# The gather's token rows kept in column order, with the stationary operand at every eighth column

## The reference, cut to what matters

```python
def grouped_moe(h, router_w, router_bias, w_gate, w_up, w_down):
    xt = h.reshape(B * T, D)                       # 256 tokens x 1024
    aff = jax.nn.sigmoid((xt @ router_w).astype(jnp.float32))
    ...                                            # 2 experts of 16 for each token, and their shares
    hg = jnp.einsum('nd,edf->nef', xt, w_gate)     # 1024 -> 512 for each expert
    hu = jnp.einsum('nd,edf->nef', xt, w_up)
    act = jax.nn.silu(hg) * hu * gates[:, :, None].astype(hg.dtype)
    out = jnp.einsum('nef,efd->nd', act, w_down)   # 512 -> 1024
```

## Time and profile before

| | us |
|---|---|
| median of 3 runs (1164.02 to 1165.67) | 1165.38 |
| the profiled execution, its own time | 1164.87 |
| its span, first to last instruction | 1163.1 |
| PE busy | 1073.0 (92%) |
| PEld busy | 743.2 (64%) |
| DVE busy | 562.8 (48%) |
| ACT busy | 419.8 (36%) |
| POOL busy | 89.3 (8%) |

### The profile page before, as it was taken

One profiled execution on the slowest core, in us unless ns is written; L12 is line 12 of the kernel. 1 busy time (PEld: TensorE's weight loads), 2 busy tenths in 40 slices (PEclk: granted clock), 3 DMA queues, 4 the chain that ended last, 5 costly groups with the idle time before them and its releaser, 6 DMA issues.

```text
span 1163.1 us, 15867 instructions
## 1 busy us (share of the span) xinstructions
PE 1073.0 (92%) x6103; PEld 743.2 (64%) x6103; DVE 562.8 (48%) x1054; ACT 419.8 (36%) x750; POOL 89.3 (8%) x114
## 2 busy tenths in 40 slices
PE   6999998999999999896999999979889699999995
PEld 5899977899999787674444443358767544444332
DVE  5754375766666556756222222274684722222224
ACT  5355435545455345732111111143474321111111
POOL 1200000000000011510000000011151000000000
PEclk9999998999999998997999999989989899999998
DMA  8743353545554442338999999943241889999993
GB/s 297 253 145 109 100 189 110 181 160 201 185 186 170 139 131 107 110 137 347 421 420 420 420 420 418 418 158 119 78 149 70 361 349 421 418 420 420 420 420 132
DMA packets 81684, 294.55 MB, mean 253 GB/s; under 512 B 7253, under 2 KB 40387, under 8 KB 56915
## 3 DMA queue, kind: packets, MB, share of 16 engines
q1 hardware_dynamic: 79456, 289.29, 64.6%
q10 hardware_dynamic: 1394, 2.18, 0.5%
q0 software_dynamic: 768, 2.19, 0.5%
HBM read 292.59 MB, written 1.05 MB: 252 GB/s over the span
## 4 chain that ended last, share of the span: by engine, by line
PE 78%; DVE 9%; DMA 5%; ACT 5%; issue 3%; POOL 0%; ACTq 0%; DVEq 0%; SPq 0%; POOLq 0%
PE bank L2278 16%; PE bank L2287 8%; PE bank L1846 7%; PE bank L1848 7%; PE bank L1847 7%; PE bank L1901 4%; PE bank L1902 4%; PE bank L1903 4%; PE bank L1776 4%; PE bank L2265 3%; PE bank L2310 3%; PE bank L1935 2%; DMA k_t<-in_w_up 2%; DMA raw<-in_w_in 2%; PE bank L1919 2%
## 5 line engine op out<-in xcount | busy, mean ns | idle before, releaser
L1092 DVE TENSOR_TENSOR lo<-raw,hi 128x2048 fp32r<-128x2048 f32 (+3 forms) x79 | 168.4, 2149 | 71.1 <-ACT hi L688 70.7
L688 ACT CAST hi<-raw 128x2048 fp32r<-128x2048 f32 (+3 forms) x79 | 140.1, 1795 | 50.8 <-PE bank L1848 47.2
L1901 PE MATMUL bank<-xs,hi 128*128 128x256 f32 x448 | 129.2, 288 | 6.5 <-DVE lo L1092 3.5
L1846 PE MATMUL bank<-hi,xs 128*128 128x512 f32 (+2 forms) x312 | 125.8, 403 | 8.2 <-DVE gates L1586 5.5
L1321 DVE TENSOR_TENSOR proj<-bank,proj 64x512 f32<-64x512 f32 x32 | 34.6, 1082 | 204.1 <-PE bank L2300 191.6
L1902 PE MATMUL bank<-xs,hi 128*128 128x256 f32 x448 | 128.1, 286 | 0.0
L1903 PE MATMUL bank<-xs,lo 128*128 128x256 f32 x448 | 128.0, 286 | 0.0
L1848 PE MATMUL bank<-lo,xs 128*128 128x512 f32 (+2 forms) x312 | 119.1, 382 | 0.0
L1847 PE MATMUL bank<-hi,xs 128*128 128x512 f32 (+2 forms) x312 | 119.0, 381 | 0.0
L1901 PEld LDWEIGHTS bank<-xs,hi 128*128 128x128 f32 x448 | 87.3, 195 | 8.2 <-DVE lo L1092 4.0
L1030 ACT ACTIVATE proj<-bank 64x512 f32<-64x512 f32 x32 | 18.8, 589 | 202.4 <-PE bank L2279 202.4
(11 more groups left out here) (278 smaller groups left out, 2081.4 us busy)
## 6 DMA issues: line engine op xcount, KB each, us to landing
raw<-in_w_up SPq DMA_DIRECT2D x40, 1024.0 KB, 5.4
raw<-in_w_in SPq DMA_DIRECT2D x28, 1024.0 KB, 5.3
moe_w<-in_w_gate SPq DMA_DIRECT2D x24, 1024.0 KB, 16.1
moe_w<-in_w_up SPq DMA_DIRECT2D x24, 1024.0 KB, 17.6
moe_w<-in_w_down SPq DMA_DIRECT2D x24, 1024.0 KB, 16.4
raw<-in_w_down SPq DMA_DIRECT2D x19, 1024.0 KB, 6.7
raw<-in_w_gate SPq DMA_DIRECT2D x10, 1024.0 KB, 13.1
raw<-in_w_o SPq DMA_DIRECT2D x8, 1024.0 KB, 4.8
```

The source lines that it names most:

```text
L688: nc.scalar.copy(high(n)[:, 0:size], raw[:, n % RING, 0:size]).then_inc(S["hi_done"], 1)
L1092: tt(low(n)[:, 0:size], raw[:, n % RING, 0:size], high(n)[:, 0:size].bitcast(F32), ALU.subtract).then_inc(S["lo_done"], 1)
L1846: mm(out_, lhs_hi, rhs_hi, start=first, stop=False)
L1901: mm(dst, wh[:, k, col], x_hi, start=k == 0, stop=False)
```

## The change

`x_rows` holds the 1024 columns in their own order: the casts and subtractions read 512 adjacent elements of `x` and write 512 adjacent elements. The gather's weight load takes its 128 columns, the same 8q + c as before, at a step of 8 elements (32 bytes). Nothing else differs: the instructions, their order, their sizes and the semaphores are the same. In the numbering of the profile after the change, lines behind L83 are one lower.

```diff
-X_CHUNKS = "p (q c) -> p c q"
...
         def row_chunks(part, half, i):
-            return x_rows[:, part, half, 512 * i:512 * (i + 1)].rearrange("p (c q) -> p c q", q=P)
+            return x_rows[:, part, half, 512 * i:512 * (i + 1)]
...
         def x_chunks(half, i):
-            return x[:, half, :].rearrange(X_CHUNKS, c=DC)[:, 4 * i:4 * i + 4, :]
+            return x[:, half, 512 * i:512 * (i + 1)]
...
                 def gather_step(g, f, to):
...
                     for c in range(2):
-                        chunk = slice((2 * f + c) * P, (2 * f + c + 1) * P)
+                        chunk = slice(2 * f + c, D, DC)
...
                     # late_expert
-                                ins = mm(bank[0][:, c * SLOTS:(c + 1) * SLOTS], x_rows[:, part, half, c * P:(c + 1) * P],
+                                ins = mm(bank[0][:, c * SLOTS:(c + 1) * SLOTS], x_rows[:, part, half, c:D:DC],
```

## The result

The change makes the kernel slower: 1192.1 us median (1190.7 to 1195.3) against 1165.5 (1164.0 to 1169.8), a ratio of 1.0222 with a 95% interval of 1.0197 to 1.0248, which is 26.5 us (23.0 to 28.9 by that interval). The forecast was 1187 us, the range 1162.8 to 1196. The profiled execution has a span of 1190.1 us against 1163.1.

What follows compares the result with a forecast made beforehand. The prediction took PE to bound the kernel, even where DMA is full. Layer norm -1.45, gather ahead 2 x 2.7 and beside the experts 2 x 9.0 made +22 us on 1164.9: 1187 us, range 1162.8 to 1196.

Steps and rivals of the forecast that it cites:

- What bounds: Expert stretches: PE is the path although DMA is full; PE waits for a transfer only 1.2 us a layer.
- Rival C: Expert stages: full DMA hides the gather steps there, only the 32 pairs ahead are paid, 1169 us; chance 0.05.
- Casts and subtractions: L1006 and L1291: 0.59 and 0.44 us less each, 8 times; only the earlier layer norm counts, -1.45 us.
- Weight loads: Gather's L2265: a strided load takes 0.224 us a pair, 0.106 us more per warm pair.
- three bounds: Gather's strided load: 0.25 and 0.24 us from ACT's and DVE's strided reads, 0.20 from 1.8 times PE's own 0.112.
- The gather ahead: 32 pairs a layer before the experts: 2.0 to 3.4 us more, taken as 2.7.
- whatever the clock: 32 pairs ahead of the experts: a load of 0.24 us at either clock level gives 7.4 us instead of about 5.5.
- Beside the experts: 12 steps of 8 pairs a layer: 96 x 0.106 = 10.2 us, less 1.2 us of DMA wait, 9.0.
- The sum: Whole kernel: -1.45 + 2 x 2.7 + 2 x 9.0 = +22 us on 1164.9, giving 1187 us.
- Rival A: Gather's L2265: the weight port takes the step at price 0, 1163.4 us, not slower; chance 0.28.
- Rival B: Gather's loads: each weight is fetched more than once, 0.448 us a pair warm, 1245 us; chance 0.07.

Runs made afterwards that it cites:

- beside_only: Changed kernel, but only the 96 pairs beside the experts load every 8th column, the 32 ahead adjacent ones; ratio 1.0166 to the kernel before.
- ahead_only: Changed kernel, but only the 32 pairs ahead of the experts load every 8th column, those beside them adjacent ones; ratio 1.0042 to the kernel before.
- casts_only: Changed kernel, but the gather loads adjacent columns as before, leaving only the contiguous casts and subtractions; 1166.5 us against 1167.7 for the kernel before.
- moving4: Kernel before, but the moving operand of the down projection's 264 matmuls is read at every 4th element (16 bytes); 1229.5 us, measured once.
- step3: Kernel before, but the gather's weight load takes every 3rd column (12 bytes); 1182.6 us, measured once.
- loads_only: Kernel before, casts and subtractions still strided, but the gather's weight load takes every 8th column; 1195.5 us, ratio 1.0235.
- adj4: Kernel before, but rows stored with 4 neighbouring columns together, so the gather's load takes every 4th column (16 bytes); ratio 1.0159.

## Why the prediction was right

**What bounds.** Right. PE is the path in both places of the gather, and the transfers gave back only PE's one wait a layer (-2.4 us). Rival C, that the full DMA hides the steps beside the experts, is refuted by `beside_only` (19.4 us) and `ahead_only` (4.9 us).

**Casts and subtractions.** Right in size (634 and 686 ns against 618 and 693) and in what reaches the path: 0.74 us in the first layer (0.78 less 0.04), of -1.45 forecast for both. The 0.9988 forecast for `casts_only` lies within its interval.

**Weight loads.** Right in kind, short in size: the surcharge on a warm pair was put at 0.106 us and is 0.12. The prediction took "twice PE's own load, 0.224 us a pair"; it is 0.24. The value was chosen between three bounds (0.20, 0.24, 0.25), and the one from DVE's strided read, 1.9 ns an element, would have been right. That is a match of numbers and no shared price: the moving operand pays 0.90 ns (`moving4`). Doubling PE's own 0.112 took the strided load for the adjacent one done twice. But a strided one takes 0.243 us at the lower clock and 0.241 at the higher, so it is limited by something that does not follow PE's clock. That it comes near twice the adjacent load is luck of this step and no rule: `step3` takes 0.172 us, 1.5 times.

**The gather ahead.** 2.37 us more a layer against 2.7 in the sum. Of its two cases the one "whatever the clock" (7.4 us) was it: the cold pairs are 0.243 apart, not 0.427, and 0.243 is little over the 0.211 that they had. The 7.4 itself is a little short, because it priced the warm part at 0.224; the stretch takes 7.97.

**Beside the experts.** 12 x 0.98 = 11.8 us a layer, against 10.2 in the sum: again the 0.016 us a pair.

**The sum.** With 0.241 in place of 0.224 and the right cold case the same terms give 24.4, so 1189. These 24.4 us lie within the interval of the measured difference (23.0 to 28.9), and the trace has the rest before the first layer norm and between the layers, where no strided load stands. The errors partly cancel: the gather ahead was put 0.7 us too high for both layers and the steps beside the experts 3.2 too low, and the rest of the distance to 1192 was in no term.

**Rival A** needed a load of under 0.142 us. `loads_only` and `adj4` rule that out. The rule in the Trainium skill's "TensorE: Matmul & The Clock Gate", LDWEIGHTS, that a load's time follows from its columns alone, holds here for steps of 1 and 2 and fails from 3 on (0.172, 0.230). The Trainium skill's "Advanced Engine Details and Errata", Memory Cachelines, has lines of 16 bytes and asks for two accesses in each. By this case's traces step 2 is free (0.120 us) and step 4 is not (0.230), which agrees. **Rival B** (0.448 us) did not occur.

## What to carry to other kernels

A layout that is awkward to write is paid once for each element written, one that is awkward to load is paid at every load: here 8 casts and 8 subtractions saved 0.5 us each, and 256 loads paid 0.12 each, on the busier engine. Before a stationary operand is read at a step, compare the load (1.8 ns for each 16-byte piece it touches, in these runs) with the matmul beside it: beside 512 columns almost nothing of it shows (0.245 us a pair against 0.227), beside 256 all that exceeds the matmul does. Interleaving in pairs of 4-byte elements keeps two of them in each piece and costs neither side anything worth naming.

## What was not expected of the hardware

A strided weight load takes the same time at either level of the clock (0.243 and 0.241 us a pair), while pairs with an adjacent one take 0.211 and 0.118. Beside 256 columns the low clock therefore costs the strided pairs nothing. A step of 64 bytes is a little cheaper (0.218) than 16 or 32 (0.230, 0.236). The moving operand pays 0.90 ns for a column at a step of 16 bytes, half of the 1.8 ns that the weight load pays for the same step.
